# The feed-forward stage of an encoder layer as two passes, each product formed from seven half products

## What is computed

```
x  = x + concatenate([att, ssm]) @ w_out
h2 = rmsnorm(x, norm2_w)
y  = x + (silu(h2 @ w_gate) * (h2 @ w_up)) @ w_down
```

## Time and profile before

| what | value |
|---|---|
| median of 3 runs | 3603.54 us (3599.82 to 3607.7) |
| span of the profiled execution | 3602.8 us |
| own time of that execution outside its span | not listed; the runs shown lie within 4.2 us of the median |
| PE busy | 3407.4 us, 95% |
| DVE, ACT, POOL busy | 1565.8, 1200.6, 649.1 us |
| data moved | 434.88 MB, mean 121 GB/s |
| output projection | about 1498 to 1759 us of the span |
| feed-forward | about 1759 to 3602.8 us |

### The profile page before, as it was taken

One profiled execution on the slowest core, in us unless ns is written; L12 is line 12 of the kernel. 1 busy time (PEld: TensorE's weight loads), 2 busy tenths in 40 slices (PEclk: granted clock), 3 DMA queues, 4 the chain that ended last, 5 costly groups with the idle time before them and its releaser, 6 DMA issues.

```text
span 3602.8 us, 47503 instructions
## 1 busy us (share of the span) xinstructions
PE 3407.4 (95%) x16682; PEld 2803.3 (78%) x16682; DVE 1565.8 (43%) x2072; ACT 1200.6 (33%) x2072; POOL 649.1 (18%) x622
## 2 busy tenths in 40 slices
PE   7999999969998699799699999999999999999999
PEld 6787877757776588688588888888888888888887
DVE  3444535546665789733333233323332233223322
ACT  3333434436775355422222222222222222222221
POOL 1101001013332367411111101110111011101110
PEclk9999999989999899899899999999999999999999
DMA  5354554573331322455533443344333433443333
GB/s 180 129 193 164 169 167 162 170 164 76 84 84 34 89 65 70 135 170 180 153 93 96 130 130 98 93 124 132 95 103 119 138 93 93 122 137 102 93 99 99
DMA packets 644237, 434.88 MB, mean 121 GB/s; under 512 B 118288, under 2 KB 576064, under 8 KB 643952
## 3 DMA queue, kind: packets, MB, share of 16 engines
q1 hardware_dynamic: 634656, 404.93, 39.0%
q0 software_dynamic: 6624, 23.72, 2.0%
q10 hardware_dynamic: 2880, 5.24, 0.4%
HBM read 349.74 MB, written 84.82 MB: 121 GB/s over the span
## 4 chain that ended last, share of the span: by engine, by line
PE 50%; DMA 0%; ACT 0%; DVE 0%; SPq 0%; issue 0%
PE f_ps_gate L61 6%; PE f_ps_gate L63 6%; PE f_ps_down L63 6%; PE f_ps_down L61 6%; PE f_ps_gate L62 6%; PE f_ps_down L62 6%; PE f_ps_up L63 6%; PE f_ps_up L61 6%; PE f_ps_up L62 6%; PE f_ps_turn L2310 1%; DMA f_raw<-w_up_dram 0%; ACT f_yT L2182 0%; DVE f_w_lo L2221 0%; ACT f_w_hi L2162 0%; SPq L2105 0%
## 5 line engine op out<-in xcount | busy, mean ns | idle before, releaser
L2221 DVE TENSOR_TENSOR f_w_lo<-f_raw,f_w_hi 128x2048 fp32r<-128x2048 f32 (+1 forms) x190 | 471.0, 2479 | 534.8 <-ACT f_w_hi L2162 534.8
L2162 ACT CAST f_w_hi<-f_raw 128x2048 fp32r<-128x2048 f32 (+1 forms) x190 | 320.5, 1687 | 763.0 <-PE f_ps_up L63 536.8
L61 PE MATMUL f_ps_gate<-f_h_hi,f_w_hi 128*128 128x512 f32 x880 | 343.6, 390 | 25.2 <-DVE f_w_lo L2221 24.4
L2234 DVE TENSOR_TENSOR f_hid<-f_g_silu,f_ps_up 128x512 f32<-128x512 f32 x110 | 75.6, 688 | 658.2 <-PE f_ps_up L63 658.2
L61 PE MATMUL f_ps_down<-f_hid_hi,f_w_hi 128*128 128x512 f32 x880 | 345.8, 393 | 0.0
L62 PE MATMUL f_ps_gate<-f_h_lo,f_w_hi 128*128 128x512 f32 x880 | 343.1, 390 | 0.0
L63 PE MATMUL f_ps_gate<-f_h_hi,f_w_lo 128*128 128x512 f32 x880 | 343.0, 390 | 0.0
L63 PE MATMUL f_ps_down<-f_hid_hi,f_w_lo 128*128 128x512 f32 x880 | 343.0, 390 | 0.0
L62 PE MATMUL f_ps_down<-f_hid_lo,f_w_hi 128*128 128x512 f32 x880 | 342.6, 389 | 0.0
L61 PE MATMUL f_ps_up<-f_h_hi,f_w_hi 128*128 128x512 f32 x880 | 342.3, 389 | 0.0
L62 PE MATMUL f_ps_up<-f_h_lo,f_w_hi 128*128 128x512 f32 x880 | 342.3, 389 | 0.0
(11 more groups left out here) (223 smaller groups left out, 6373.0 us busy)
## 6 DMA issues: line engine op xcount, KB each, us to landing
i_raw<-w_in_dram SPq DMA_DIRECT2D x60, 1024.0 KB, 5.5
f_raw<-w_gate_dram SPq DMA_DIRECT2D x110, 512.0 KB, 4.0
f_raw<-w_up_dram SPq DMA_DIRECT2D x110, 512.0 KB, 5.2
f_raw<-w_down_dram SPq DMA_DIRECT2D x80, 384.0 KB, 3.9
f_raw<-w_down_dram SPq DMA_DIRECT2D x80, 320.0 KB, 3.1
i_cx<-xbcT SPq DMA_DIRECT2D x40, 258.0 KB, 3.0
i_x_t<-x_dram SPq DMA_DIRECT2D x20, 512.0 KB, 6.0
xbcT<-i_ev SPq DMA_DIRECT2D x40, 256.0 KB, 2.9
```

Of the source, the lines that this page charges most:

```text
L61: pe.matmul(out, w_hi, x_hi, start=first, stop=False)
L2162: act.copy(w_hi[:, par, 0:size], raw[:, par, 0:size]).then_inc(slot_hi_done[par], 1)
L2221: dve.tensor_tensor(w_lo[:, par, 0:size], raw[:, par, 0:size], w_hi[:, par, 0:size].bitcast(F32), ALU.subtract).then_inc(slot_lo_done[par], 1)
L2234: dve.tensor_tensor(hid[:, par], g_silu[:, par], ps_up[:, par], ALU.mult) \
```

## The change

The feed-forward's matrices are cut into halves in each dimension, and each product of 2 x 2 half blocks is formed from seven products of sums (Strassen's scheme) instead of eight.

Output projection: token tiles are paired by `PAIR_TILES`, so that the two tiles of a pair lie in different halves. For each pair DVE makes four combinations of h2 (`combine`), POOL stores seven operand tiles into `h_ops` (3 from h2, 4 combinations) instead of two h2T tiles. POOL also combines the four quarters of w_down once (`combine_wd`, 11 times, 4 subtractions of 128x512) and stores them to `wd_ops`; SP loads those quarters. The hardware loop is unrolled.

First pass (`ffn_up_phase`): 1280 columns (half of the tokens) in blocks of 512, 512 and 256; in each, 11 pairs of hidden tiles, for gate (mat 0) and up (mat 1) seven products of 4 x 3 matmuls. The host lays the weight out as `w_ffn`, 1 MB per pair and matrix with 8 KB per partition. DVE makes four weight sums and seven low parts for each matrix, combines the product banks, multiplies by the gate, and makes four combinations of the hidden tiles; seven operands are stored to `hid_ops`. POOL does nothing here.

Second pass (`ffn_down_phase`): 3 blocks of 4, 3 and 3 token-tile pairs, 7 products, 11 steps each; a step loads a 128x512 tile of w_down (or a combination) and the tokens of one hidden operand, splits both, and makes 3 matmuls of 512 columns for each of the 4 or 3 token tiles. Tokens are stationary, so that no transposes are needed. A ring of 10 steps holds raw, high and low parts.

The core of the diff:

```diff
+FP = KF // 2
+PAIR_TILES = [(q, q + 4) for q in range(4)] + [(q + 4, q + 8) for q in range(4, 8)] + [(q + 8, q + 10) for q in (8, 9)]
...
@@ out_proj_phase
+            def load_wd(kp):
+                sp.wait_ge(wd_made, 4 * kp)
+                for j in range(2):
+                    r = (j * (KF // 2) + kp) * P
+                    sp.dma_start(wd_raw[:, j], w_down[r:r + P, :].rearrange("p (l c) -> p l c", l=2)) \
+                      .then_inc(wd_loaded, 16)
-            with sp.Fori(1, PAIRS) as i:
+            load_wd(0)
+            for i in range(1, PAIRS):
                 load(i, 0)
                 load(i, 1)
+                load_wd(i)
+            load_wd(KF // 2 - 1)
...
+            def combine(i):
+                dve.wait_ge(comb_stored[buf], 64 * (i // 2))
+                dve.tensor_tensor(t1, b12, b11, ALU.subtract).then_inc(comb_made, 1)
...
             def store_h2(i, par):
+                for half, j in G_B[par]:
+                    pool.dma_start(h_ops[j, :, :, cols], h2[:, par, half * KH:(half + 1) * KH]) \
+                        .then_inc(h2_stored[par], 16)
+                if par == 1:
+                    pool.wait_ge(comb_made, 4 * i + 4)
+                    for n in range(4):
+                        pool.dma_start(h_ops[G_T[n], :, :, cols], ...)
+            def combine_wd(kp):
+                pool.wait_ge(wd_loaded, 32 * (kp + 1))
+                pool.wait_ge(wd_stored, 64 * kp)
...
             def step(now, after, before):
                 store_x1(*now)
                 if before:
                     store_h2(*before)
+                if now[1] == 1:
+                    combine_wd(now[0])
...
@@ ffn_up_phase, in place of the first half of ffn_phase
+    BLOCK_N = (TB, TB, TB // 2)
+    BANK = (0, 1, 2, 3, 0, 2, 3)
...
+            def load_h(b, j, half):
+                n = BLOCK_N[b]
+                wait(sp, h_lo_done, 2 * (SLOTS * b + j) + half - 1)
+                sp.dma_start(h_raw[:, half, :, 0:n], h_ops[j, :, 2 * half:2 * half + 2, BLOCK_AT[b]:BLOCK_AT[b] + n]) \
+                  .then_inc(h_loaded[half], 16)
...
+            def group(b, g, mat, new_h, end):
+                if not end:
+                    sums(*nxt)
+                for j in range(SLOTS):
+                    if j > 0:
+                        dve.wait_ge(product_done, SLOTS * m + j + 1)
...
+                    if not end:
+                        split_w(*nxt, j)
+                    if new_h:
+                        split_h(b + 1, j)
+                if mat == 1:
+                    combine(b, g)
...
+            def group(b, g, mat):
+                free = {0: c11_out, 1: u2_done, 2: c21_out, 3: c12_out}
+                kept = {4: p1_out, 5: u3_done, 6: c22_out}
+                for j in range(SLOTS):
+                    pe.wait_ge(w_lo_done, SLOTS * m + j + 1)
+                    if mat == 0:
+                        pe.wait_ge(h_lo_done, 2 * (SLOTS * b + j + 1))
+                    if j in free:
+                        wait(pe, free[j][mat], g)
+                    else:
+                        pe.wait_ge(kept[j][mat], g + 1)
+                    for k in range(KH):
+                        done = split_products(pe, out, w_hi[:, j, w], w_lo[:, j, w], h_hi[:, j, k, 0:n], ...)
...
@@ ffn_down_phase, in place of the second half of ffn_phase
+    RING = 10
+    BLOCKS = ((0, 4), (4, 3), (7, 3))
+    BANKS = (0, 1, 0, 1, 0, 1, 0)
+    AFTER = RING // 2
...
+                if n >= RING:
+                    sp.wait_ge(lo_done, n - RING + 1)
+                sp.dma_start(raw[:, r, 0:TB], src).then_inc(loaded[r], 16)
+                sp.dma_start(raw[:, r, TB:TB + w], hid_ops[j, k, :, first * P:first * P + w]).then_inc(loaded[r], 16)
...
+            for n in range(len(STEPS)):
+                load(n)
+                if k == FP - 1 and j in OUT:
+                    load_x1(b, j)
+                if k == FP - 2 and n > FP:
+                    if pj in OUT:
+                        store(pb, pj)
...
+                pe.wait_ge(lo_done, n + 1)
+                for t in range(BLOCKS[b][1]):
+                    done = split_products(pe, acc[:, BANKS[j], t * TB:(t + 1) * TB], hi[:, r, tok], lo[:, r, tok],
+                                          hi[:, r, 0:TB], lo[:, r, 0:TB], ...)
```

More of the change, by code:

```diff
@@ L54, in phase_semaphores, with split_products @@
     nc.all_engine_barrier()
[L57 to L63, removed]
+def split_products(pe, out, w_hi, w_lo, x_hi, x_lo, first, last, resumed=False):
+    pe.matmul(out, w_hi, x_hi, start=first, stop=False, skip_group_check=resumed)
+    pe.matmul(out, w_hi, x_lo, start=False, stop=False, skip_group_check=resumed)
+    return pe.matmul(out, w_lo, x_hi, start=False, stop=last, skip_group_check=resumed)
 def in_proj_phase(nc, x, w_in, cols, qk_w, bias_pad, copies, ident_dram, q_s, k_s, v_s, z_s, dtT, xbcT, xcT):
@@ L1846, in out_proj_phase @@
         h2_stored = two("h2_stored")
+        comb_made = sem("comb_made")
+        comb_stored = two("comb_stored")
+        wd_loaded = sem("wd_loaded")
+        wd_made = sem("wd_made")
+        wd_stored = sem("wd_stored")
         def steps(eng, step):
@@ L1852, in body @@
                 step((i, 1), None if last else (i + 1, 0), (i, 0))
[L1853 to L1856, removed]
+            for i in range(PAIRS):
+                body(i, i == 0, i == PAIRS - 1)
         def tokens(i, par):
-            return bass.ds((2 * i + par) * P, P)
+            t = PAIR_TILES[i][par]
+            return slice(t * P, (t + 1) * P)
         block = ctx.enter_context(nc.Block())
@@ L1953, in step @@
                 scale(*now)
+                if before and before[1] == 1:
+                    combine(before[0])
             dve.memset(eps[:], EPS).then_inc(eps_made, 1)
@@ L2057, in ffn_phase @@
[L2057 to L2062, removed]
+        h_hi = sb("h_hi", [P, SLOTS, KH, TB], F32R)
+        h_lo = sb("h_lo", [P, SLOTS, KH, TB], F32R)
+        h_raw = sb("h_raw", [P, 2, 2, TB])
+        w_raw = sb("w_raw", [P, 2, 4, KH * P])
@@ L2073, in ffn_phase @@
[L2073 to L2088, removed]
+        product_done = sem("product_done")
+        p1_out = two("p1_out")
@@ new lines, in ffn_up_phase, with wait @@
+        u2_done = two("u2_done")
+        u3_done = two("u3_done")
+        c11_out = two("c11_out")
+        c12_out = two("c12_out")
+        c21_out = two("c21_out")
+        c22_out = two("c22_out")
+        silu_done = sem("silu_done")
+        hid_made = sem("hid_made")
+        comb_made = sem("comb_made")
+        hid_stored = [sem(f"hid_stored{c}") for c in range(4)]
+        comb_stored = sem("comb_stored")
+        def wait(eng, s, n):
+            if not isinstance(n, int) or n > 0:
+                eng.wait_ge(s, n)
@@ L2090, in ffn_phase, with pairs @@
+        def pairs(eng, body):
+            for b in range(3):
+                if b == 0:
+                    body(b, 0, 0, False, False)
+                lo = 1 if b == 0 else 0
+                with eng.Fori(lo, FP - 1) as i:
+                    body(b, i, b * FP + i, False, False)
+                body(b, FP - 1, b * FP + FP - 1, b < 2, b == 2)
         block = ctx.enter_context(nc.Block())
@@ L2128, in store_y @@
[L2128 to L2155, removed]
+            def load_w(g, i, mat):
+                wait(sp, w_lo_done, SLOTS * (2 * g + mat - 1))
+                sp.dma_start(w_raw[:, mat].rearrange("p q c -> p (q c)"),
+                             w_ffn[i, mat].rearrange("p q k c -> p (q k c)")).then_inc(w_loaded[mat], 16)
@@ new lines, in body @@
+            def body(b, i, g, new_h, end):
+                if not end:
+                    following = 0 if new_h else i + 1
+                    load_w(g + 1, following, 0)
+                    load_w(g + 1, following, 1)
+                if new_h:
+                    for j in range(SLOTS):
+                        for half in range(2):
+                            load_h(b + 1, j, half)
+                store(b, g, i)
+            load_w(0, 0, 0)
+            for j in range(2):
+                load_h(0, 0, j)
@@ L2157, in _ @@
+            load_w(0, 0, 1)
+            for j in range(1, SLOTS):
+                for half in range(2):
+                    load_h(0, j, half)
+            for b in range(3):
+                for i in range(FP):
+                    body(b, i, b * FP + i, i == FP - 1 and b < 2, i == FP - 1 and b == 2)
+            for c in (C11, C21, C22):
+                sp.wait_ge(hid_stored[c], 16 * 3 * FP)
+            sp.wait_ge(comb_stored, 64 * 3 * FP)
         @block.scalar
         def _(act):
-            def split_slot(n, par, size):
-                act.wait_ge(slot_loaded[par], 32 * (n + 1))
-                act.wait_ge(slot_done[par], n)
-                act.copy(w_hi[:, par, 0:size], raw[:, par, 0:size]).then_inc(slot_hi_done[par], 1)
@@ L2211, in _, with body @@
+            def body(b, i, g, new_h, end):
+                group(b, g, 0, False, False)
```

(42 more changed lines are left out.)

582 lines of the change are left out of this document (372 added, 210 removed).

## The result

The changed kernel takes 3503.54 us (median of 4 runs, 3500.29 to 3507.04) against 3605.56 for the kernel before on the same chip: 0.9718 of it, 95% interval 0.9706 to 0.973, a gain of about 102 us. The forecast was 3520.

The account below looks back on a forecast made before the run. PE's matmul issue rate was taken to bound the kernel. Terms from the output projection's last turn sum to 1758.5 against 1851.4 us, -93; +10 in the output projection makes -83, so 3602.8 becomes 3520 us, range 3450 to 3590.

Parts of the forecast that it names:

- block changes: First pass, between blocks: refilling seven h slots delays PE 17 us, 12 for the half-width block; together 29 us (bounds 5 and 45).
- output projection, to its last turn: Output projection stage: fuller POOL queue, more DMA and SP's waiting add 10 us (bounds 0 and +50).
- its end to the first pass: After the output projection's last turn: POOL's last combinations and stores add 21 us (bounds 15 and 35) to 7.8.
- start of the first pass beyond work: First pass start: h slots arrive 5.6 us apart through two raw buffers, 36 us beyond 19.1 of work (bounds 16 and 45).
- full blocks: First pass, two 512-column blocks: 3696 matmuls at 0.227 us, 839 us, with DVE's 28.7 us per pair hidden behind PE's 38.1.
- half-width block: First pass, 256-column block: DVE slower than PE, 24 us per pair, 264 us (bounds 211 and 347).
- between the passes: From the first pass's last product: combinations, stores and barrier 11 us, first load and split 8; 19 us.
- second pass with waits and clock: Second pass: 2310 matmuls 524 us with DMA hidden, 5 us waits at two block boundaries, 5 us low clock over two starts.
- PE's rate: Feed-forward matmul spacing on PE: 0.227 us per 512 columns, 0.12 taken for 256 columns.
- the rival at PE's rate: Small block runs at PE's rate, 211 us, and h chains are half as long (-32 us): 3435 us, chance 0.09.
- The wait of SP in load_wd: Output projection: SP waits for POOL's wd_made before issuing the next mix, some 22 us against a 23.6 deadline; stage +10 us.
- Waits in every pair: Output projection, sign of being wrong: PE waits for o_mix_lo in every pair, 5 us each, the +50 bound.

Follow-up runs that it names:

- the quarters: Changed kernel with the first pass's h operands loaded in quarters of a slot through four raw buffers instead of halves through two: 3476.58 us.

## Why the prediction was right

The direction, the main mechanism (fewer matmuls at an unchanged rate) and the size held; one step, the block changes, left out a cost. Step by step, forecast and measured in us of the span:

| step | forecast | measured |
|---|---|---|
| first product of the output projection | 0 | -2.6 (1506.66, before 1509.24) |
| output projection, to its last turn | +10 | +10.1 (250.3, before 240.2) |
| its end to the first pass | 28.8 | 26.6 |
| start of the first pass beyond work | 36 | 41 |
| full blocks | 839 | 838 (3696 x 0.2267) |
| block changes | 29 | 43 |
| half-width block | 264 | 240 (220 us for 1695 recorded matmuls, 168 a pair) |
| between the passes | 19 | 12.1 |
| second pass with waits and clock | 534 | 530.8 |
| tail | 8.5 | 8.0 |
| sum from the last turn before (1751.4) | 1768 | 1747 |

The start and the changes are what is left over: the start is the first group's end, about 1845.9, less the phase's start and 19.1 of work; the changes are what remains of the 1162 us of the first pass.

- **PE's rate** was right to the percent at 512 columns, and at 256: the starts are 0.120 us apart, the value taken. Each has its own weight load. By the Trainium skill (TensorE: Matmul & The Clock Gate, The mechanism) a weight load overlaps running matmuls only when the row group differs, which the prediction worked out to 0.214; that does not hold here.

```profile
2817.00 0.28 PE L67 MATMUL u_acc<-u_h_hi,u_w_lo 128*128 128x256 f32 x1
2817.12 0.28 PE L65 MATMUL u_acc<-u_h_hi,u_w_hi 128*128 128x256 f32 x1
```

- **The half-width block** is held by DVE, as said, though narrowly. A pair takes 21.8 us. DVE works 20.2 of them, the rest is mostly hand-offs between dependent operations, and it never waits for PE; PE works 20.3 and waits 1.5 for u3 (L2360), 15 of 220 us in all, and at 384 columns these waits vanish. The term was 24 us too dear: the 240 measured lie midway between the forecast's 264 and the 211 of the rival at PE's rate. What was mis-sized is the 22.7 us of DVE work, the sum of 40 full listed durations. Consecutive operations overlap a little, so that a subtraction listed at 0.69 starts 0.60 to 0.61 us after the one before (1790.25, 1790.86, 1791.46 in the timeline). Here listed durations overstate the time of operations in a row, as they do with matmuls. In the full blocks it is the same: DVE works 26 of PE's 38 us, where 29 were forecast.
- **The start** was 5 us too cheap because a slot took 6.7 to 7.2 us and not 5.6. The term that was wrong is the landing: the prediction took the 2.8 us of a 256 KB transfer, but half a slot is 512 KB and lands in 3.9 (the DMA line beside the quarters); with 1.1 us more the forecast's own sum gives 6.7. That this chain sets the start is shown by the quarters.
- **Block changes**, 29 against 43, are the term that was most too cheap. PE's idle there is 19.3 us at the first change (5.59, 1.00, 9.72 and 2.97) and 13.8 in the 50 us around the second; the rest fits the granted clock, 0.88 and 0.83 in those stretches. The forecast had the idle nearly right and charged the clock only to the two starts.
- **POOL's tail** was right in its sum: the last combination ends the phase, 26.6 us after the last turn's end, where 28.8 were forecast. Its parts cancel: five h stores took 3.7 us instead of 6 and the last four stores 2.2 instead of 4.4, and 3.0 us of waiting for the stores of the combination before were not foreseen. Moving the combinations takes 9 us off the gap before the first pass, leaving them out 12; the rest of either gain is the wait in load_wd.
- **The wait of SP in load_wd** was foreseen, and its 10 us were met within 0.1, which is luck at bounds of 0 and 50. PE waited for o_mix_lo 8 times, 8.3 us in all. Waits in every pair had been named as a sign of being wrong, at 5 us each; they came nearly as often and cost about 1 us each.
- **The pass change** was overpriced by 7 us: last matmul 2947.63, SP's first load 2953.57, first matmul 2959.73.

The errors partly cancelled: -24 and -7 against +14 and +5; the other lines add up to -9. That the sum fell within 21 us is in part luck.

## What to carry to other kernels

A scheme that trades matmuls for sums pays here because the vector engine's work per tile (low parts and sums of weights, whatever the block's width) nearly fits beside the products even in the narrowest block; count it for the narrowest block, not for the mean, and choose block widths by measured spacings. Before giving up on the rest of an ideal saving, look at the ends of phases: an engine that runs one item more than there are steps, and a refill through two large raw buffers instead of four smaller ones, cost 50 us here and were mended without leaving any work out. If an expected gain does not show, look in the trace whether its mechanism worked and something else took it back.

## What the runs showed of the hardware

- Spacing of float32r matmuls with their own weight loads, full clock: 0.2267 us at 512 columns, 0.2033 at 448, 0.1733 at 384, 0.120 at 256. In cycles of 2.4 GHz that is the columns plus 32, except for 448, with 40. The Trainium skill (TensorE: Matmul & The Clock Gate, Back-to-back issue gap) gives, for the gap of an isolated matmul, 518 cycles at 512 columns and 262 at 256, 26 fewer than measured here. Why 448 is dearer stays open.
- A vector subtraction of 1.22 us stretched to 4.67 us beside POOL's tensor operations, which ran back to back from 1608.91 to 1614.95; over the stage its mean was 2.70 us, and 1.22 without them. Additions that read PSUM stayed at 0.684.

```profile
1609.12 4.67 DVE L1947 TENSOR_TENSOR o_mix_lo<-o_mix,o_mix_hi 128x1024 fp32r<-128x1024 f32 x1 [0.48 <-ACT o_mix_hi L1914]
...
1612.78 2.17 POOL L2037 TENSOR_TENSOR o_wd_comb<-o_wd_raw,o_wd_comb 128x512 f32<-128x512 f32 x1
```

- Transfers with rows of 2 KB and 1.5 KB from one issuing engine held 371 GB/s over 140 us.
